# Decode work of layer 0 as steps between the units of the prompt attention, and another order of norm and output tiles in front of layer 1's feed-forward

## What is computed

```python
q_lat = einsum(q[..., :NOPE], w_uk);  c_kv = rms_norm(kv_a[..., :KVL], kv_norm)
rows = concatenate([c_kv, k_pe], -1)                     # output: 288 columns for each token
lat = blockwise causal softmax attention over rows       # the decode tokens: over their paged cache and their row
mla_out = einsum(lat, w_uv)
o, s_fin = gla_chunked(gq, gk, gv, log_a, s0)            # decode: s = exp(log_a) * s0 + k v,  o = q s
o = rms_norm(o, g_norm) * silu(g_r)
out = concatenate([mla_out, o], -1) @ w_out
```

## Time and profile before

| | |
|---|---|
| three runs | 3632.26, 3633.6, 3640.36 us |
| median | 3633.6 us |
| profiled execution | 3640.52 us, span 3638.7 us |
| mean granted clock of PE in it | 0.968 |
| PE busy | 3399.5 us (93%) |
| DVE, ACT, POOL busy | 46%, 17%, 3% |

### The profile page before, as it was taken

How to read it: one execution, slowest core, us unless ns; L and a number is a source line. 1 busy time by engine, 2 the same in 40 slices (tenths; PEclk the granted TensorE clock), 3 DMA queues, 4 the chain that set the end, 5 groups by cost and what they waited for, 6 DMA issues and landing times. The chain is left out here.

```text
span 3638.7 us, 45085 instructions
## 1 busy us (share of the span) xinstructions
PE 3399.5 (93%) x18216; PEld 2510.8 (69%) x18216; DVE 1668.2 (46%) x3894; ACT 630.5 (17%) x1628; POOL 95.0 (3%) x138
## 2 busy tenths in 40 slices
PE   9999888766889999999999999999987999999997
PEld 5675565654557777776777767767764777777676
DVE  0216455688254333357760212122456433335777
ACT  1214223233130000000030111111223000000002
POOL 0000000011000000000000000000220000000000
PEclk9999799899899999999999999999988999999998
DMA  3120100298321111111221111122210111011122
GB/s 134 35 58 1 46 33 1 108 351 325 128 82 47 46 37 43 46 61 64 78 87 46 60 56 55 56 73 69 79 67 23 47 46 46 35 46 61 64 89 100
DMA packets 63531, 266.58 MB, mean 73 GB/s; under 512 B 6288, under 2 KB 24728, under 8 KB 52352
## 3 DMA queue, kind: packets, MB, share of 16 engines
q1 hardware_dynamic: 55072, 176.94, 14.0%
q0 software_dynamic: 8288, 87.30, 6.4%
HBM read 246.29 MB, written 17.93 MB: 73 GB/s over the span
## 5 line engine op out<-in xcount | busy, mean ns | idle before, releaser
L512 PE MATMUL ps<-arena 128*128 128x344 f32 (+1 forms) x4928 | 1083.1, 383 | 22.4 <-ACT arena L560 12.0
L512 PEld LDWEIGHTS ps<-arena 128*128 128x128 f32 x4928 | 833.6, 192 | 272.6 <-issue 26.0
L766 PE MATMUL ps<-arena 128*128 128x344 f32 (+1 forms) x2464 | 539.8, 382 | 1.5 <-DVE arena L685 1.5
L766 PEld LDWEIGHTS ps<-arena 128*128 128x128 f32 x2464 | 415.3, 191 | 126.7 <-DVE arena L685 3.4
L1945 PE MATMUL ps<-arena 128*128 128x344 f32 x1152 | 354.3, 465 | 15.6 <-ACT arena L352 5.7
L1945 PEld LDWEIGHTS ps<-arena 128*128 128x128 f32 x1152 | 221.3, 195 | 134.7 <-issue 26.3
L216 PE MATMUL ps<-arena 128*128 128x344 f32 x672 | 198.5, 459 | 8.9 <-DMA arena<-in_w_a 8.9
L1956 PE MATMUL ps<-arena 128*128 128x256 f32 (+1 forms) x864 | 206.4, 396 | 0.0
L1956 PEld LDWEIGHTS ps<-arena 128*128 128x128 f32 (+1 forms) x864 | 178.9, 264 | 23.5 <-issue 6.2
L562 ACT ACTIVATE arena<-arena 128x688 f32<-128x688 f32 (+1 forms) x88 | 55.7, 633 | 756.5 <-DVE arena L624 756.5
L216 PEld LDWEIGHTS ps<-arena 128*128 128x128 f32 x672 | 129.8, 194 | 76.8 <-DMA arena<-in_w_a 8.9
(11 more groups left out here) (322 smaller groups left out, 3662.0 us busy)
## 6 DMA issues: line engine op xcount, KB each, us to landing
arena<-in_w_fi SPq DMA_DIRECT2D x44, 1024.0 KB, 4.8
arena<-in_w_fo SPq DMA_DIRECT2D x16, 1536.0 KB, 6.4
arena<-in_w_fo SPq DMA_DIRECT2D x16, 1280.0 KB, 5.7
arena<-in_w_out_a SPq DMA_DIRECT2D x24, 512.0 KB, 3.5
arena<-in_w_qk SPq DMA_DIRECT2D x24, 512.0 KB, 3.6
arena<-in_c SPq DMA_DIRECT2D x6, 2048.0 KB, 12.3
arena<-in_x SPq DMA_DIRECT2D x6, 1376.0 KB, 10.3
arena<-in_w_a SPq DMA_DIRECT2D x14, 512.0 KB, 3.5
```

The source lines that it names most:

```text
L512: mm = pe.matmul(ps[:, BANK[p], 0:HALF[s]], prod[j][p][0], prod[j][p][1], start=(j == 0), stop=(j == 3))
L766: mm = pe.matmul(ps[:, BANK[p], 0:HALF[s]], prod[p][0], prod[p][1], start=(j == 0), stop=(j == NKP - 1))
```

## The change

In layer 0 the decode work behind `pe_gla` is cut into 23 steps (`FILL`), and `pe_mla` and `dve_mla` do one of them behind every second unit, u = 2, 4, ... 46: keys; the state of one decode token, 8 times; out in two halves; norm; one tile of rows, 9 times; query; new row. All steps use PSUM bank 7, and the outputs of the attention bank 6 alone, so `values(u)` waits for the output of unit u-1 rather than u-2. The meeting of the engines at phase 8 is dropped for PE, ACT and DVE; keys and values are made directly behind `pe_gla`. The decode queries of GLA are first copied to `GQD`, since the outputs overwrite `gq`. POOL's first gathers wait for all nine outputs of this part of the layer. In layer 1 the order of tiles, norm steps and decode turn is another, in all three lists, and DVE's first weight sums of the feed-forward (`dve_w_in(1, 0)`) move ahead of `dve_t_in`, which now stands in one piece behind the last chunk's sum.

The diff, cut to its core (each line eight columns to the left); left out are the steps' bodies that only change the bank, `dve_cache_row`, the old forms of the loops, and moved buffers:

```diff
 def act_ln_scale(act, n, c, l, s):
+    act_ln_rstd(act, n, c)
+    act_ln_gain(act, n, c, l, s)
+def act_ln_rstd(act, n, c):
...
     act.activation(LN_R[n % 2], LN_R[n % 2], ACT.Exp, scale=-0.5).then_inc(ln_rstd, 1)
+def act_ln_gain(act, n, c, l, s):
...
 def dve_ffn_in(dve, l):
     n_ln = 2 * l
-    dve_w_in(dve, l, 0)
+    if l == 0:
+        dve_w_in(dve, l, 0)
...
+GQD = at(A_CONST + CONST_SIZE - 48, 2, DEC)
...
+def pe_gla_decode_state(pe, b):
+    pe.wait_ge(gs_km, b + 1)
+    if b:
+        pe.wait_ge(gs_stc, 2 * b)
+    for pr in range(2):
+        pe.matmul(ps[:, 7, 2 * pr * P:2 * pr * P + 2 * P], KM[0:DEC, b, pr * P:pr * P + P],
+                  GV[0:DEC, NT, 2 * pr * P:2 * pr * P + 2 * P], start=True, stop=True).then_inc(gs_st, 1)
+def pe_gla_decode_out(pe, hh):
+    pe.wait_ge(gs_stc, 2 * DEC)
+    if hh:
+        pe.wait_ge(gs_o, 2)
+    r = slice(64 * hh, 64 * hh + 64)
+    for pr in range(2):
+        for b in range(DEC):
+            mm = pe.matmul(ps[:, 7, pr * DEC + b:pr * DEC + b + 1], SG[r, b, pr, :], GQD[r, pr, b:b + 1],
+                           start=True, stop=True)
+    mm.then_inc(gs_o, 1)
...
+def dve_gla_decode_state(dve, b):
+    dve.wait_ge(state_in, 64)
+    dve.wait_ge(gs_st, 2 * b + 2)
     for pr in range(2):
         for hh in range(2):
             r = slice(64 * hh, 64 * hh + 64)
+            ins = dve.scalar_tensor_tensor(out=SG[r, b, pr, :], in0=SG[r, b, pr, :], scalar=ELA[r, pr, b:b + 1],
+                                           in1=ps[r, 7, (2 * pr + hh) * P:(2 * pr + hh + 1) * P],
+                                           op0=ALU.mult, op1=ALU.add)
+        ins.then_inc(gs_stc, 1)
...
+def pe_cache_row(pe, tt):
+    m = P if tt < NT else DEC
+    s = slice(tt * P, tt * P + m)
+    if tt:
+        pe.wait_ge(r_cp, tt)
+    else:
+        pe.wait_ge(gn_r, NT + 1)
+    for k in range(2):
+        pe.transpose(ps[0:m, 7, k * P:k * P + P], PB[:, T_CKV + k, s], ident[:, :])
+    pe.transpose(ps[0:m, 7, KVL:KVD], PB[64:96, T_MISC, s], ident[64:96, 64:96]).then_inc(r_ps, 1)
...
 V = at(A_GV, NT + 1, 512)
-o = A_TMP + NH * T
+o = A_TMP + GP * KVD
 KH = [at(o + q * SEQ, SEQ) for q in range(2)]; o += 2 * SEQ
-assert o <= A_END
+assert o <= A_END - 4 * T
 SP_ = [at(A_PB + T_CQ * T + q * SEQ, SEQ) for q in range(2)]
 PT = at(A_PB + T_CQ * T + 2 * SEQ, SEQ)
 O = at(A_PB + T_GQ * T, NT, 512)
...
     sem(x) for x in ("m_s", "m_mask", "m_p", "m_t", "m_tc", "m_o", "m_oc"))
+d_cp, D_CP0 = kh_pe, 2
+FILL = [("keys", 0)] + [("state", b) for b in range(DEC)] + [("out", 0), ("out", 1), ("norm", 0)]
+FILL += [("row", tt) for tt in range(NT + 1)] + [("query", 0), ("new", 0)]
+def fill_at(u):
+    return FILL[u // 2 - 1] if u % 2 == 0 and 0 < u // 2 <= len(FILL) else ("", 0)
+LAST_FILL = 2 * len(FILL)
...
             pe.wait_ge(v_cp, NT)
-        if u >= 2:
-            pe.wait_ge(m_oc, u - 1)
+        if u:
+            pe.wait_ge(m_oc, u)
         for j in range(i + 1):
-            mm = pe.matmul(ps[:, 6 + u % 2, 0:64], PT[:, j * P:(j + 1) * P], V[:, j, h * 64:h * 64 + 64],
+            mm = pe.matmul(ps[:, 6, 0:64], PT[:, j * P:(j + 1) * P], V[:, j, h * 64:h * 64 + 64],
...
         mm.then_inc(m_o, 1)
+    def fill(what, x):
+        if what == "keys":
+            pe_gla_decode_keys(pe)
+        if what == "state":
+            pe_gla_decode_state(pe, x)
+        if what == "out":
+            pe_gla_decode_out(pe, x)
+        if what == "norm":
+            pe_gnorm(pe, NT)
+        if what == "row":
+            pe_cache_row(pe, x)
+        if what == "query":
+            pe_decode_query(pe)
+        if what == "new":
+            pe_decode_row(pe)
+    pe.wait_ge(q_act, 3 * NH)
+    pe.wait_ge(q_dve, 3 * NH)
     keys(0)
+    pe.wait_ge(gn_r, NT - 1)
+    pe_mla_values(pe, range(6))
+    pe.wait_ge(v_cp, 6)
+    pe_gnorm(pe, NT - 1)
+    pe.wait_ge(kh_cp, 1)
+    keys(1)
+    pe.wait_ge(gn_r, NT)
+    pe_mla_values(pe, range(6, NT))
+    pe.wait_ge(g_atc, NGLU)
+    pe.wait_ge(g_oc, NGLU)
+    pe.wait_ge(g_stc, NGLU)
+    scores(0)
     for u, (h, i) in enumerate(MU):
-        if u == 0:
-            scores(0)
-            pe.wait_ge(kh_cp, 1)
-            keys(1)
...
             values(u - 1)
+        fill(*fill_at(u))
...
         act.wait_ge(m_iv, u + 1)
-        act.mul(O[:, i, h * 64:h * 64 + 64], ps[:, 6 + u % 2, 0:64], m_inv[:, u % 2:u % 2 + 1]).then_inc(m_oc, 1)
+        act.mul(O[:, i, h * 64:h * 64 + 64], ps[:, 6, 0:64], m_inv[:, u % 2:u % 2 + 1]).then_inc(m_oc, 1)
...
             output(u - 2)
+        if u and fill_at(u - 1) == ("out", 1):
+            act.wait_ge(gs_o, 4)
+            act_gnorm_squares(act, NT)
+        if u and fill_at(u - 1) == ("norm", 0):
+            act_gnorm(act, NT)
...
 def dve_mla(dve):
     for q in range(2):
-        dve.wait_ge(row_out[q], 16 * (NT // 2))
-    for q in range(2):
         dve.tensor_copy(KH[q][64:96, :], PB[64:96, T_MISC, 0:SEQ]).then_inc(kh_pe, 1)
+    dve.tensor_copy(GQD, gq[:, :, SEQ:T])
+    def fill(what, x):
+        if what == "keys":
+            dve_gla_decode_keys(dve)
+        if what == "state":
+            dve_gla_decode_state(dve, x)
+        if what == "out":
+            dve_gla_decode_out(dve, x)
+        if what == "row":
+            dve_cache_row(dve, x)
+        if what == "query":
+            dve_decode_query(dve)
+        if what == "new":
+            dve_decode_row(dve)
     def keys(h):
...
     keys(0)
+    dve_mla_values(dve, range(6))
+    link("dve", dve, dve_gnorm(dve, NT - 1))
+    keys(1)
+    dve_mla_values(dve, range(6, NT))
     mask(0)
-    keys(1)
...
         finish(u)
+        fill(*fill_at(u))
+        if u and fill_at(u - 1) == ("norm", 0):
+            link("dve", dve, dve_gnorm(dve, NT))
...
             keys(h + 2)
+    for q in range(2):
+        dve.wait_ge(row_out[q], 16 * (NT // 2))
+    dve.wait_ge(out_done, 16 * 9)
...
     pool.wait_ge(pidx_ok, NG)
-    enter(pool, 8)
-    pool.wait_ge(out_done, 16 * 8)
+    pool.wait_ge(out_done, 16 * 9)
...
     pe_out_c(pe, 1, 5)
+    pe_out_c(pe, 1, 6)
+    pe_ln_var(pe, 2, 0)
+    pe_out_c(pe, 1, 7)
     pe_decode_turn(pe)
-    pe_out_c(pe, 1, 6)
-    pe_out_c(pe, 1, 7)
     pe_out_c(pe, 2, 0)
-    pe_ln_var(pe, 2, 0)
-    pe_out_c(pe, 2, 2)
-    pe_out_c(pe, 2, 4)
     pe_ln_sum(pe, 2, 1)
-    for n in (6, 1, 3, 5):
+    for n in (2, 4, 6, 1):
...
     pe_ln_var(pe, 2, 1)
-    pe_out_c(pe, 2, 7)
+    for n in (3, 5, 7):
+        pe_out_c(pe, 2, n)
 def act_last(act):
...
             act_decode_soft(act)
-    act_ln(act, 2, 0, 1, 0)
-    act_ln(act, 2, 1, 1, 0)
+    act_ln_squares(act, 2, 0)
+    act_ln_rstd(act, 2, 0)
+    act_ln_squares(act, 2, 1)
+    act_ln_gain(act, 2, 0, 1, 0)
+    act_ln_rstd(act, 2, 1)
+    act_ln_gain(act, 2, 1, 1, 0)
...
 def dve_last(dve):
...
     dve_ln_centre(dve, 2, 0)
-    dve_decode_copy(dve)
...
     dve_ln_squares(dve, 2, 0)
+    dve_out_c(dve, 1, 6)
+    dve_decode_copy(dve)
+    dve_out_c(dve, 1, 7)
+    dve_out_c_sum(dve, 1)
     dve_decode_out(dve)
-    for n in (6, 7):
-        dve_out_c(dve, 1, n)
-    dve_out_c_sum(dve, 1)
+    dve_ln_centre(dve, 2, 1)
     dve_ln_scale(dve, 2, 0)
-    for n in (0, 2, 4):
-        dve_out_c(dve, 2, n)
-    dve_ln_centre(dve, 2, 1)
-    for n in (6, 1):
+    for n in (0, 2):
...
     dve_ln_squares(dve, 2, 1)
-    for n in (3, 5):
+    for n in (4, 6, 1):
...
     dve_ln_scale(dve, 2, 1)
-    dve_out_c(dve, 2, 7)
-    dve_t_in(dve, 2, 0, range(2))
+    for n in (3, 5, 7):
+        dve_out_c(dve, 2, n)
     dve_out_c_sum(dve, 2)
-    dve_t_in(dve, 2, 0, range(2, 4))
+    dve_w_in(dve, 1, 0)
+    dve_t_in(dve, 2, 0, range(4))
...
     pe_gla(pe)
-    pe_gla_decode_keys(pe)
-    pe_gnorm(pe, NT - 1)
-    pe.wait_ge(gn_r, NT)
-    pe_mla_values(pe, range(4))
-    pe_gla_decode_states(pe)
-    pe_mla_values(pe, range(4, NT))
-    pe_gla_decode_out(pe)
-    pe.wait_ge(q_act, 3 * NH)
-    pe_cache_rows(pe)
-    pe.wait_ge(v_cp, NT)
-    pe_gnorm(pe, NT)
     pe.sem_inc(phase["pe"], 8)
-    for k, f in ((8, pe_mla), (9, pe_pages)):
-        enter(pe, k)
-        f(pe)
+    pe_mla(pe)
+    enter(pe, 9)
+    pe_pages(pe)
...
     act_gnorm(act, NT - 1)
-    act.wait_ge(gs_o, 2)
-    act_gnorm_squares(act, NT)
-    act_gnorm(act, NT)
-    act.wait_ge(gn_r, NT + 1)
     act.sem_inc(phase["act"], 8)
-    for k, f in ((8, act_mla), (9, act_pages)):
-        enter(act, k)
-        f(act)
+    act_mla(act)
+    enter(act, 9)
+    act_pages(act)
...
     dve_gla(dve)
-    dve_gla_decode_keys(dve)
-    dve_gnorm(dve, NT - 1)
-    dve_mla_values(dve, range(4))
-    dve_gla_decode_states(dve)
-    dve_mla_values(dve, range(4, NT))
-    dve_gla_decode_out(dve)
-    link("dve", dve, dve_cache_rows(dve))
-    link("dve", dve, dve_gnorm(dve, NT))
     dve.sem_inc(phase["dve"], 8)
-    for k, f in ((8, dve_mla), (9, dve_pages), (10, dve_mo_decode)):
-        enter(dve, k)
-        f(dve)
+    dve_mla(dve)
+    enter(dve, 9)
+    dve_pages(dve)
+    enter(dve, 10)
```

(46 more changed lines are left out.)

59 lines of the change are left out of this document (22 added, 37 removed).

## The result

| kernel | median of its runs, us | range | ratio to before, 95% interval |
|---|---|---|---|
| before, beside the runs of the changed kernel | 3632.5 (20 runs) | 3627.2 to 3642.3 | |
| changed | 3624.4 (20 runs) | 3613.2 to 3641.2 | 0.9979 [0.9969, 0.9989] |

The change makes the kernel faster by 8 us, 0.2%, where I had forecast 20 (3613.6). The sign is right and the size less than half of what I forecast: the time lies in the wide range (3596 to 3628), but outside the forecast's own 3605 to 3621. The profiled execution of the changed kernel is the slowest of its 20, 3641.16 us (span 3639.2), so its span stands beside the 3638.7 of before as if nothing had been won. A stretch of it can be compared with the same stretch of before, its total can't.

A forecast was written before the change was run, and what follows sets the result against it. TensorE (PE), busy 93% of the span, bounds the kernel. Prologue 49.5 us less, fills 23.5 and clock 3.0 back, layer 1 3.0 later: 20 off the median 3633.6 gives 3613.6; forecast 3605 to 3621, wide range 3596 to 3628.

The forecast's parts named there:

- Part 1: Layer 0, last GLA product to unit 0's transposes: shortened to keys, values and one norm, 49.5 us less.
- Part 2: Layer 0's attention: the 23 decode steps put behind every second unit cost 23.5 us, bounds 13 and 35.
- keys step: Attention, unit 2: PE 0.3 us, but VectorE's 8 masks and a copy come before the next mask; costs 2.0 us.
- state steps: Attention, units 4 to 18: eight steps of 0.85 us on PE, partly in holes, with late copies; 7.2 us in all.
- Out steps: Attention, units 20 and 22: 3.3 us of PE each, one less a 0.67 hole; 5.9 us in all.
- Query and new row: Attention, units 44 and 46: 5.0 us, the query's 48 passes priced at the 0.104 us of an out pass.
- the norm: Attention, unit 24: no PE work, but ScalarE's two table loads and two operations delay unit 26's exponential; 1.6 us.
- The lower bound of this part: Fills in the attention: PE's work alone 22.8 us; if 9.7 of holes take it up and VectorE is hidden, 13.
- One output bank: Attention: values wait for the output of the unit before; taken as 0, 12 us if 40 units lost 0.3.
- the clock term: Attention: two of the three out and query steps lower the clock for some 3.5 us each, 3.0 us; bounds 0 and 16.
- the clock swings in the attention: Rival, chance 0.18: the steps bring the lower clock for some 40 us, costing 17 us instead of 3; about 3628.
- Part 3: Layer 1 junction: new order 2.7 us earlier at full clock, but three PE holes cost 5.7 in clock; 3.0 us later.

The follow-up runs named there:

- e1: The changed kernel with layer 1's order as before, so layer 0's change alone: 3616.8 us, ratio 0.9951 to before.
- e12: The changed kernel with out and query steps cut to 2, 2 and 3 small products, and 4, 4 and 6 unread dense products in front: 3612.0 us.
- e6: The changed kernel with each out step in four pieces and the query step in six, one piece behind each unit: 3612.1 us.
- e7: The kernel before with layer 1's new order alone, and five unread products of 344 columns in each of its three PE holes: 3632.6 us.
- e2: The kernel before with layer 1's new order alone: 3638.2 us, ratio 1.0013 to before.

## Why the prediction was off by 12 us of its 20

**Part 1, 49.5 us less:** right, 49.1. The pieces agree within 0.6: keys(0) 4.81 for 5.4, six value tiles 10.57 for 10.25, the wait 0.78 for 0.9, norm 1.12 for 0.85, keys(1) 3.65 and the last values 3.70 for 3.4 each.

**Part 2, the fills, 23.5:** right in size. The keys step gave the hole of 1.62 behind 0.38 of PE's work, 2.0 as forecast. Four state steps in a head at full clock cost 31.2 less 27.5, 3.7, for a forecast of 3.6 (1.45 + 1.45 + 0.7). It came out that way by two errors that cancel: the step takes PE 1.13, not 0.85, and the copy is 0.2 late behind two of the steps, 0.6 behind one. Out steps are 3.73 for 3.3 each. Query and new row are 6.5 for 5.0 here, but the clock is in that: in e1, at full clock, they are 3.91 and 0.30, so that the 5.0, worked out from the out passes, was too much. At the norm the waits of 0.90 and 1.01 stand where before had one of 1.13, 0.8 more, for 1.6. As a sum: the attention grew by 41.7 us, with 49 us more at the lower level; at 0.43 per us that is 21, and 20.6 are left for the fills, 3 less than forecast. The lower bound of this part was mis-added: its parts as listed make 21.9 us of PE's work, not 22.8. One output bank cost nothing, as forecast: no wait on the outputs stands ahead of any values.

**The step that failed is the clock term: "I take two of the three to lower it for some 3.5 us each: 3.0".** Its price, 0.43 us of time per us at the lower level, holds: the fastest and the slowest of the 20 runs are 27.9 us apart at mean clocks of 0.975 and 0.966, 0.009 x 3639 x 2 = 66 us more at the lower level, 0.43 again (a line through all 20 gives 0.40). The duration was wrong. I booked 7 us at the lower level, two falls that recover after 3.5. One fall did: the 4 us behind the first out step. The clock stayed down for 11 us behind the second and for 25 in and behind the query step, until the wide keys of the next head had run. That makes 37 us at the lower level in the profiled execution and 24 in that of e1, at 0.43 some 16 and 10 us of time. Dense work in their place (e12) and the same products in small lots (e6) each give 12 us back by the median: the term is about 12, not 3. With that alone the sum is 20 less 9, 11 faster.

The reading under that term was wrong too. I took the out and the query products for those "under which the clock was at 0.50 before". The earlier trace rows shows that for the query alone. In the same trace the out products ran at 0.89, and it was the 9 us behind them that stood at 0.50, with PE busy for 7.9 of them:

```profile
420.50:427.00 6.50, 6.50 (x65) 6.50 (x64) 0.69 (x1) 0.00 (x0) 0.00 (x0) 0.89 0.00 0
427.00:436.30 9.30, 7.86 (x29) 4.05 (x28) 3.48 (x10) 1.51 (x2) 0.00 (x0) 0.50 0.28 95
```

Why the clock came back after 4 us behind one out step and not behind the other, and why the query step fell in one execution and not in the other, stays open.

This is the rival that I gave 0.18, *the clock swings in the attention*, in its mechanism: it named 40 us at the lower level, and the attention had 49 more than before in the profiled execution. In its other terms the forecast held, and the measured 3624.4 lies between its 3613.6 and the rival's 3628. The Trainium skill (TensorE: Matmul & The Clock Gate, A second HAM failure mode) has such swings come from short pauses between groups of wide products. In this kernel the pauses of 1.1 us in a head of before run at 1.00, and lots of narrow products with PE busy throughout brought the swings about. If the pauses were the cause, e12, which has the same ones, would have kept the loss; it gave 12 us of it back. What lowers the clock in head 0, which e12 has at 0.70 too, is another matter and not found.

**Part 3, layer 1, 3.0 later:** right in sign and mechanism, 1 too small. Three holes of 4.10, 4.24 and 4.16 for 4.4, 4.3 and 4.4; at full clock 2.3 earlier (e7) for 2.7; the clock takes 7.0 where I had 5.7. At the third product it is 4.7 later, in the total 4.1 (e2).

So: 49.1 less, 23.5 and 12 given back in the attention, 4.1 in layer 1, which is 9.5 faster, against 8.1 measured. It is put together from numbers with some 3 us of doubt each, so that it closes this well is in part luck: with the 20.6 of the profiled execution for the fills it is 12.4 faster.
